# Two tiles at a time on TensorE: taking turns between PSUM banks in an encoder's channel mixer

## What is computed

```
h = rms_norm(x, g_ffn) * (1.0 + scale_f) + shift_f
u = depthwise_conv_centred(h @ w_up, conv_w, conv_b)      # w_up: 1024 x 5632, conv of width 3 over positions
val, gate = jnp.split(u, 2, axis=-1)
y = (jax.nn.silu(gate) * val) @ w_down                    # w_down: 2816 x 1024
return x + gate_f * y
```

## Time and profile before

| what | value |
|---|---|
| median of 3 runs | 1195.87 us (1193.13 to 1203.88) |
| span of the profiled execution | 1192.1 us |
| matmuls / weight loads on TensorE | 6300 / 6300 |
| mean granted TensorE clock over the span | 0.986 of full speed |
| packets of DMA queue q1 | 36.8% of 16 engines' span |

### The profile page before, as it was taken

The page is one execution under the profiler, slowest core; times in us unless marked ns, Lnnn a source line. Parts: engine busy times, 40 slices in busy tenths (PEclk is TensorE's granted clock), DMA queues, the critical chain, the costliest instruction groups (busy, mean ns, idle before and its releaser), DMA issues.

```text
span 1192.1 us, 18794 instructions
## 1 busy us (share of the span) xinstructions
PE 1161.1 (97%) x6300; PEld 997.5 (84%) x6300; DVE 730.3 (61%) x1481; ACT 535.7 (45%) x866; POOL 564.8 (47%) x768
## 2 busy tenths in 40 slices
PE   9999998999999999999999999999999999999997
PEld 8897787998888888888789979789888888888886
DVE  6787996767766677767665438646775134412345
ACT  5347675354431344234454687625543134422432
POOL 2477400655555445644666540054555544454462
PEclk8899998999999999999999999999999999999999
DMA  9853233424445345544433202222343322332322
GB/s 346 311 174 110 89 106 107 141 72 144 173 139 201 142 154 176 194 144 174 141 116 116 72 1 89 89 89 71 124 141 106 106 88 88 106 106 75 102 89 71
DMA packets 43979, 151.55 MB, mean 127 GB/s; under 512 B 5122, under 2 KB 7810, under 8 KB 43908
## 3 DMA queue, kind: packets, MB, share of 16 engines
q1 hardware_dynamic: 43908, 150.64, 36.8%
HBM read 148.52 MB, written 2.10 MB: 126 GB/s over the span
## 4 chain that ended last, share of the span: by engine, by line
PE 39%; issue 30%; POOL 19%; POOLq 8%; DVE 3%; DVEq 1%; ACT 0%; ACTq 0%
POOL w_lo L535 17%; PE ps L614 12%; PE ps L615 12%; PE ps L620 12%; POOLq L536 6%; DVE ada_prod L1584 1%; PE ps L718 1%; POOL qb_tmp L579 1%; POOLq L592 1%; POOL qb L584 0%; DVE h_lo L1627 0%; PE ps L737 0%; POOLq L589 0%; PE ps L726 0%; DVE xn L1618 0%
## 5 line engine op out<-in xcount | busy, mean ns | idle before, releaser
L535 POOL TENSOR_TENSOR w_lo<-w_raw,w_hi 128x256 fp32r<-128x256 f32 x712 | 530.3, 777 | 602.1 <-ACT w_hi L1105 578.5
L614 PE MATMUL ps<-h_hi,w_hi 128*128 128x512 f32 (+1 forms) x960 | 348.9, 363 | 5.1 <-DVEq L1537 3.1
L615 PE MATMUL ps<-h_lo,w_hi 128*128 128x512 f32 (+1 forms) x960 | 346.4, 361 | 0.0
L620 PE MATMUL ps<-h_hi,w_lo 128*128 128x512 f32 (+1 forms) x960 | 346.3, 361 | 0.0
L1105 ACT CAST w_hi<-w_raw 128x1024 fp32r<-128x1024 f32 x178 | 183.2, 1047 | 184.6 <-PE ps L614 183.6
L614 PEld LDWEIGHTS ps<-h_hi,w_hi 128*128 128x128 f32 x960 | 181.1, 189 | 38.7 <-DVEq L1537 5.0
L1781 DVE SCALAR_TENSOR_TENSOR u_sb<-ps,par,u_sb 128x510 f32<-128x510 f32 x176 | 131.8, 749 | 123.1 <-ACT u_sb L1333 110.1
L620 PEld LDWEIGHTS ps<-h_hi,w_lo 128*128 128x128 f32 x960 | 181.2, 189 | 27.6
L615 PEld LDWEIGHTS ps<-h_lo,w_hi 128*128 128x128 f32 x960 | 181.2, 189 | 26.6
L614 PE MATMUL ps<-a_hi,w_hi 128*128 128x512 f32 (+1 forms) x400 | 146.4, 366 | 3.4 <-DVEq L1571 2.4
L620 PE MATMUL ps<-a_hi,w_lo 128*128 128x512 f32 (+1 forms) x400 | 145.5, 364 | 0.0
(11 more groups left out here) (156 smaller groups left out, 1370.2 us busy)
## 6 DMA issues: line engine op xcount, KB each, us to landing
w_raw<-w_slots SPq DMA_DIRECT2D x178, 512.0 KB, 3.5
ada_raw<-ada_slots SPq DMA_DIRECT2D x88, 512.0 KB, 3.7
shift<-shift_slots SPq DMA_DIRECT2D x8, 512.0 KB, 14.3
x_tok<-x_rows SPq DMA_DIRECT2D x4, 512.0 KB, 9.6
x<-x_t SPq DMA_DIRECT2D x4, 512.0 KB, 15.0
y_t<-x SPq DMA_DIRECT2D x3, 512.0 KB, 2.9
y_t<-x SPq DMA_DIRECT2D x1, 256.0 KB, 3.0
y_t<-x SPq DMA_DIRECT2D x2, 128.0 KB, 2.7
```

What stands on the lines that cost most here:

```text
L535: nc.gpsimd.tensor_tensor(w_lo[:, j, c], w_raw[:, j, c], w_hi[:, j, c].bitcast(F32), ALU.subtract)
L614: hh = mm(out, stat[0], mov[0], start=first, stop=False)
L615: hl = mm(out, stat[0], mov[1], start=False, stop=False)
L620: return mm(out, stat[1], mov[0], start=False, stop=last)
```

## The change

The loop over pairs and the loop over the later down tiles no longer finish one tile before the next. A new function, `two_tiles`, makes two tiles together: for each block of the contraction and each of the three kinds of product it issues one matmul for the first tile and one for the second, so that neighbours write different PSUM banks. Only for the last block are the first tile's three matmuls issued, then the second's. The waits for both tiles' weights and both banks stand ahead of the first matmul. `slot_free` is raised by the first matmul of all, and again by the second tile's first matmul of the last block. Number and kind of the matmuls are the same; the peeled pairs, down tiles 0 and 1 and the halves in `norm_tail` are as they were, as is everything on the other engines.

```diff
+            def two_tiles(outs, js, hi, lo, n, fulls):
+
+                def one(i, p, k):
+                    w, m = ((w_hi, hi), (w_hi, lo), (w_lo, hi))[p]
+                    return mm(outs[i], w[:, js[i], k * P:k * P + P], m[:, k, :], start=(k == 0 and p == 0),
+                              stop=(k == n - 1 and p == 2))
+
+                for k in range(n - 1):
+                    for p in range(3):
+                        for i in range(2):
+                            last = one(i, p, k)
+                            if (k, p, i) == (0, 0, 0):
+                                last.then_inc(slot_free, 1)
+                for i in range(2):
+                    first = one(i, 0, n - 1)
+                    if i == 1:
+                        first.then_inc(slot_free, 1)
+                    one(i, 1, n - 1)
+                    one(i, 2, n - 1).then_inc(fulls[i], 1)
@@ the loop over pairs
                                 key = ("up", g, e, half)
                                 pe.wait_ge(split_done, 4 * it + (L * SLOTS + S_UP[g] + 2 * e + half + 1))
                                 wait_free(pe, L, key, it)
-                                j = (L * SLOTS + S_UP[g] + 2 * e + half) % RING
-                                for k in range(KD):
-                                    last = product(ps[:, bank(key), :],
-                                                   [r[:, j, k * P:k * P + P] for r in (w_hi, w_lo)],
-                                                   [r[:, k, :] for r in (h_hi, h_lo)], k == 0, k == KD - 1, int(k == 0))
-                                last.then_inc(full[bank(key)], 1)
+                            at = L * SLOTS + S_UP[g] + 2 * e
+                            banks = [bank(("up", g, e, half)) for half in range(2)]
+                            two_tiles([ps[:, b, :] for b in banks], [(at + half) % RING for half in range(2)],
+                                      h_hi, h_lo, KD, [full[b] for b in banks])
@@ the down tiles
-                    for m in range(2, KD if g < len(GROUPS) - 1 else TAIL):
-                        down_tile(L, g, m, range(n), 1)
+                    for m in range(2, KD if g < len(GROUPS) - 1 else TAIL, 2):
+                        keys = [("down", g, m), ("down", g, m + 1)]
+                        js = [slot(L, S_DOWN[g] + m + i) for i in range(2)]
+                        for key in keys:
+                            wait_free(pe, L, key)
+                        two_tiles([ps[:, bank(key), :] for key in keys], js, a_hi, a_lo, n, [full[bank(key)] for key in keys])
```

## The result

The change makes the kernel slower. The median is 1273.27 us (1271.82 to 1275.33, 4 runs), beside 1199.65 us (1193.13 to 1203.88, 4 runs) for the kernel before: a ratio of 1.063 on record, 95% interval 1.059 to 1.068 (the two medians alone give 1.061). The span of the profiled execution grew from 1192.1 to 1270.0 us, by 77.9. The forecast was 1263, with a range from 1235 to 1285.

A forecast was written before the change was run, and what follows sets the result against it. TensorE, busy 97% of the span, was taken as the bound. Stands of 57.6 us on the profiled 1192.1, plus 3.8 from span to median, gave 1253.5; 10 of lost clock made 1263, range 1235 to 1285.

The forecast's parts named there:

- order of matmuls and banks: All 2568 changed matmuls: alternating banks changes nothing in their price, 0; bounds nothing and 34.2 us of gain.
- steady pairs and pairs with two adaLN slots: Loop over up pairs: weights 0.41 us late every second pair, 5.7 us; two adaLN slots in layer 0, 6 us.
- behind the peeled pairs: First loop pair of group 0: TensorE waits 4.7 us for GpSimd's low part in each layer, 9.4 us.
- down pairs, layer 0: Groups 0 and 1: TensorE waits for banks VectorE empties, 4.4 us twice a group, more ahead of tile 2; 21.2 us.
- down pairs, layer 1: Groups 0 and 1: bank waits without an adaLN slot, 1.50 us twice a group, 0.93 ahead of tile 2; 7.9 us.
- last groups: Last group of each layer: waits for last activation, tile 1's bank and updates before the half tiles; 3.7 each, 7.4 us.
- clock: Six stands of 4.4 to 4.7 us may lower TensorE's clock afterwards: 10 us, bounds nothing and 20.7.
- The chain of a pair: Steady up pairs: held cast, reads, taps, low part end at E + 10.95 (E: next matmul could start); 0.41 us late.
- short stands count too: Rival, chance 0.13: ten stands of 1.5 us or so also lower the clock, long ones at their bound; 1284 us.
- the bank was the brake on the matmuls: Rival, chance 0.08: changing banks saves 13.3 ns per matmul, -34 us, with 9 us more waits; 1238 us.
- the clock holds: Rival, chance 0.22: dense work on both sides of the stands may keep the full clock; 1253 us.
- the change doesn't bite: Rival, chance 0.04: neighbours cost the same and engines hand over earlier than read, so nothing changes; 1196 us.

The follow-up runs named there:

- early_cast: Changed kernel, but ScalarE casts the high part of the gate tile's weights for the pair after next ahead of reading the current pair: 1260.91 us (1.053).
- four_banks: Changed kernel, but down tiles go through banks 4, 5, 2, 3 instead of 4, 5: 1228.59 us (1.027).

## Why the prediction was right, and where not

The distances between starts divide the growth of the two mixers, 49.2 and 25.5 us (from the end of the peeled first halves to the last sum), into 56.7 of longer stands, 14.4 of lower clock and some 3.6 of small delays. 3.2 us lie outside the mixers.

| step | forecast | measured |
|---|---|---|
| order of matmuls and banks | 0 (to -34.2) | 0: 0.2267 us a start in either order |
| steady pairs and pairs with two adaLN slots | 5.7 + 6 | 9.4 |
| behind the peeled pairs | 9.4 | 9.1 (2 x 4.57) |
| down pairs, layer 0 | 21.2 | 21.0 |
| down pairs, layer 1 | 7.9 | 9.4 |
| last groups | 7.4 | 7.7 |
| stands together | 57.6 | 56.7 |
| clock | 10 (0 to 20.7) | 14.4 |
| small delays in the mixers; outside them | none | 3.6; 3.2 |

**The chain of a pair** came as forecast. A pair of the kernel after (E = 335.91, ScalarE, VectorE, GpSimd) and two starts that it delayed:

```profile
335.65 1.05 ACT L1127 CAST w_hi<-w_raw 128x1024 fp32r<-128x1024 f32 x1 [3.04 <-PE ps L626]
336.60 1.44 ACT L1355 ACTIVATE u_sb<-ps,par 128x512 f32<-128x512 f32 x2
337.41 3.29 DVE L1803 SCALAR_TENSOR_TENSOR u_sb<-ps,par,u_sb 128x510 f32<-128x510 f32 x4 [2.43 <-ACT u_sb L1355]
344.02 2.83 POOL L535 TENSOR_TENSOR w_lo<-w_raw,w_hi 128x256 fp32r<-128x256 f32 x4 [4.41 <-ACT w_hi L1127]
...
302.72 0.72 PE L626 MATMUL ps<-h_hi,w_hi 128*128 128x512 f32 x2 [0.17 <-POOLq L537]
324.91 0.72 PE L626 MATMUL ps<-h_hi,w_hi 128*128 128x512 f32 x2 [0.16 <-POOLq L537]
```

Cast at E - 0.26 (forecast - 0.25), reads at + 0.69 (+ 0.70), taps to + 4.79 (+ 4.80), low part at + 10.94 (+ 10.95). A stand is 0.23 to 0.33 us and not 0.41, and every second pair has one, as forecast. Four in layer 0 are longer, 0.85 to 2.21 us, where two adaLN slots precede them. `early_cast` shows that the pairs wait for this chain: with the cast of the awaited weights no longer behind reads and taps, no stand is left. The hold at the start of the chain is seen in the first of these lines, where ScalarE stands still for 3.04 us until TensorE's L626, but no run tests it alone.

**Behind the peeled pairs** (rows 7 answer): TensorE, then GpSimd, in the kernel after.

```profile
274.33 0.28 PE L620 MATMUL ps<-h_hi,w_lo 128*128 128x256 f32 x1
279.02 1.22 PE L626 MATMUL ps<-h_hi,w_hi 128*128 128x512 f32 x2 [4.42 <-POOLq L537]
...
275.98 2.78 POOL L535 TENSOR_TENSOR w_lo<-w_raw,w_hi 128x256 fp32r<-128x256 f32 x4 [5.91 <-ACT w_hi L1127]
```

**Down pairs.** Ahead of tiles 4 and 6: 4.39, 4.40, 4.39, 4.39 in layer 0 (4.4 forecast) and 1.57 four times in layer 1 (1.50). Ahead of tile 2: 2.52 and 2.07 in layer 0; 2.70 and 1.57 in layer 1. The 2.70 was missed: VectorE has adaLN work in the pairs of layer 1's first group too (a slot at 972.78 to 975.5, ahead of the update at 976.42), which I had left at none.

**Last groups.** The sum is right, partly by luck: one cause in it is not. I put the stand ahead of tile 2 at 0.93 us for tile 1's bank. It is 1.75, in the timeline of the kernel after:

```profile
634.37 0.47 PE L614 MATMUL ps<-a_hi,w_hi 128*128 128x512 f32 x1 [1.16 <-DVE a_lo L1816]
637.57 0.70 PE L626 MATMUL ps<-a_hi,w_hi 128*128 128x512 f32 x2 [1.58 <-POOLq L537]
```

and `four_banks` left it at 1.74: it is weights. The pair wants tile 3's slot at its start, and ScalarE comes to that cast only at 633.41, behind the last pair's work. I had checked in the other groups that the weights come in time, and carried that over.

**The clock** is the term that was mis-sized, by 4.4 us. In this profile each low stretch lay nearly wholly in dense work, so "half a low stretch can lie in the stand" was wrong; and it was half as long as the 6.9 us of rows 10. The two errors cancel, so that six falls cost 9.6 us beside the 10 forecast is luck. What was left out is that shorter stands can do it too: of the five of 2.0 to 2.7 us three were followed by a fall (2.52, 1.98, 2.70), two were not (2.07, 2.21). In the second profile of the same kernel it was three again, but others: behind 2.03, 2.23 and 2.70, and not behind 2.53 and 2.06. None came behind the stands of 1.57 us. What decides between them is open; the rival "short stands count too" had them from 1.5 us up and asked for 10 us for them beside 21 for the long ones, where 4.8 and 9.6 came, and is right in its direction alone.

**Small delays.** After a stand the first start is followed by the second 0.08 to 0.10 us later than elsewhere: 377.20 to 377.74 are two starts in 0.54 us, not 0.45. With some forty stands that is most of the 3.6 us.

**Outside.** 3.0 us are the one wait in attention at 126.88 (L1770). The second profile of the same kernel does not have it, at a span of 1271.7, so the change does not need it.

The 10 us that the forecast lacked are these: 4.4 of clock, 3.6 of small delays, 3.2 outside the mixers, less 0.9 of stands. The rivals are settled by the runs. That the bank was the brake on the matmuls falls with 0.2267 us a start; that the clock holds, with the rows of the stand and the filler; that the change doesn't bite, and that it is faster, with the verdict.

## What to carry to other kernels

Making two tiles together doubles what must be ready at their start, weights and banks, and lets both banks become full at once, so look at what the second bank's emptying was hidden behind before: here that alone cost 45 us. Ask for the gain first: two rows of a pitch with and without a bank change, in the trace of the kernel before, had already shown that it is nil. And price a long stand in dense work twice, for the wait and for the slow stretch after it: here 4.4 us of waiting cost 6.0. Of the stands of 2.0 to 2.7 us three in five brought a fall, of those of 1.57 us none.

## What was unexpected

- A low stretch of the clock can lie wholly behind the stand that brings it about: in the pair shown, the granted clock was full through 4.4 us of standing still, fell 0.5 us after the restart, and stayed at 1.2 GHz for 3.4 us with TensorE busy throughout. In the second profile of the same kernel the falls of the down pairs came from 0.2 us ahead of the restart to 0.1 behind it; those of the peeled stands came 1.4 and 2.4 us ahead of it and lasted 6.8 us. So the place of the fall varies between executions, and with it its price.
- 4.18 us of narrow matmuls whose results nobody reads, in a stand of 4.39 us, kept the clock: 8.9 us for six stands, without moving a real start.
- Taking a 2.8 us slot out of a stand brought 4.6 us on average (18.4 us for four), since the fall went with it.
